# A norm's rows of roots and its sums of squares, moved behind other products on TensorE in a two-block transformer kernel

## The reference

```python
def _rmsnorm(x, gain):
    x32 = x.astype(jnp.float32)
    y = x32 * lax.rsqrt(jnp.mean(x32 * x32, axis=-1, keepdims=True) + NORM_EPS)
    return (y * gain).astype(x.dtype)
...
    for l in range(DEPTH):
        h = h + 0.5 * _swiglu(_rmsnorm(h, ffn1_norm[l]), ffn1_w_gate[l], ffn1_w_up[l], ffn1_w_down[l])
        h = h + _hybrid_mixer(_rmsnorm(h, mix_norm[l]), w_in[l], ...)
        h = h + 0.5 * _swiglu(_rmsnorm(h, ffn2_norm[l]), ffn2_w_gate[l], ffn2_w_up[l], ffn2_w_down[l])
```

## Time and profile before

| | |
|---|---|
| median of three runs | 3609.88 us (3608.93 to 3610.8) |
| the profiled execution, its own time | 3611.69 us |
| its span | 3609.8 us |
| TensorE matmul busy | 3382.9 us, 94% |
| VectorE busy | 1724.0 us, 48% |
| ScalarE busy | 1338.8 us, 37% |
| DMA | 288.05 MB, mean 80 GB/s |
| TensorE's mean granted clock | 0.967 of full speed |

### The profile page before, as it was taken

The page is one execution under the profiler, slowest core; times in us unless marked ns, Lnnn a source line. Parts: engine busy times, 40 slices in busy tenths (PEclk is TensorE's granted clock), DMA queues, the critical chain, the costliest instruction groups (busy, mean ns, idle before and its releaser), DMA issues.

```text
span 3609.8 us, 38935 instructions
## 1 busy us (share of the span) xinstructions
PE 3382.9 (94%) x15366; PEld 2744.1 (76%) x15366; DVE 1724.0 (48%) x2415; ACT 1338.8 (37%) x1897; POOL 30.5 (1%) x62
## 2 busy tenths in 40 slices
PE   8999988799999999998979999988999998999998
PEld 6888765687888888876668788877777776778887
DVE  4443454654443444344465444454445466544433
ACT  4332334343322333233434333344444456433322
POOL 0000000000000000000000000000000000000000
PEclk9999999999999999999989999998999999999999
DMA  4333211112333233322111232321211222233332
GB/s 139 100 91 98 93 59 53 32 45 90 99 93 99 91 98 96 98 83 64 55 31 42 94 99 91 97 76 41 65 47 59 71 90 72 87 102 96 100 92 66
DMA packets 107396, 288.05 MB, mean 80 GB/s; under 512 B 22912, under 2 KB 34176, under 8 KB 107216
## 3 DMA queue, kind: packets, MB, share of 16 engines
q1 hardware_dynamic: 91696, 278.70, 25.0%
q10 hardware_dynamic: 14208, 2.63, 0.4%
q0 software_dynamic: 1312, 4.25, 0.4%
HBM read 282.64 MB, written 2.88 MB: 79 GB/s over the span
## 4 chain that ended last, share of the span: by engine, by line
PE 77%; DVE 11%; ACT 9%; issue 3%; DMA 1%; ACTq 0%; DVEq 0%; SPq 0%
PE ps L722 23%; PE ps L724 22%; PE ps L723 22%; DVE wl L1830 3%; ACT wh L1289 3%; DVE mf L2014 2%; PE ps L731 2%; PE ps L1029 1%; PE ps L1024 1%; PE ps L1185 1%; DVE mf L2024 1%; PE ps L736 1%; PE ps L1167 1%; PE ps L1181 0%; ACT mf L1423 0%
## 5 line engine op out<-in xcount | busy, mean ns | idle before, releaser
L1830 DVE TENSOR_TENSOR wl<-raw,wh 128x1024 fp32r<-128x1024 f32 (+2 forms) x581 | 652.3, 1123 | 1428.1 <-ACT wh L1289 1426.4
L722 PE MATMUL ps<-hnh,wh 128*128 128x512 f32 x2712 | 1095.7, 404 | 35.5 <-DVE mf L2478 10.7
L723 PE MATMUL ps<-hnl,wh 128*128 128x512 f32 x2712 | 1070.6, 395 | 0.0
L724 PE MATMUL ps<-hnh,wl 128*128 128x512 f32 x2712 | 1070.0, 395 | 0.0
L1289 ACT ACTIVATE wh<-raw 128x1024 fp32r<-128x1024 f32 (+2 forms) x581 | 566.9, 976 | 1073.9 <-PE ps L724 1046.0
L722 PEld LDWEIGHTS ps<-hnh,wh 128*128 128x128 f32 x2712 | 520.0, 192 | 167.8 <-issue 25.5
L724 PEld LDWEIGHTS ps<-hnh,wl 128*128 128x128 f32 x2712 | 518.0, 191 | 111.3
L723 PEld LDWEIGHTS ps<-hnl,wh 128*128 128x128 f32 x2712 | 520.0, 192 | 108.3 <-issue 4.0
L722 PE MATMUL ps<-mr,wh 128*128 128x512 f32 x1300 | 514.2, 396 | 24.9 <-DVE h L1956 9.1
L723 PE MATMUL ps<-mr,wh 128*128 128x512 f32 x1300 | 509.3, 392 | 0.0
L724 PE MATMUL ps<-mr,wl 128*128 128x512 f32 x1300 | 509.2, 392 | 0.0
(11 more groups left out here) (324 smaller groups left out, 2558.0 us busy)
## 6 DMA issues: line engine op xcount, KB each, us to landing
raw<-in_w_in SPq DMA_DIRECT2D x140, 512.0 KB, 3.5
raw<-in_ffn_w_gate SPq DMA_DIRECT2D x88, 512.0 KB, 3.5
raw<-in_ffn_w_up SPq DMA_DIRECT2D x88, 512.0 KB, 3.5
raw<-in_ffn_w_down SPq DMA_DIRECT2D x64, 512.0 KB, 3.5
raw<-in_w_ffn_in SPq DMA_DIRECT2D x44, 512.0 KB, 3.5
raw<-in_ffn_w_down SPq DMA_DIRECT2D x32, 384.0 KB, 3.1
raw<-in_w_out SPq DMA_DIRECT2D x32, 256.0 KB, 2.7
raw<-in_w_out_ssm SPq DMA_DIRECT2D x32, 256.0 KB, 2.5
```

The costliest lines, as they stand in the source:

```text
L722: self.e.matmul(out, ah, bh, start=start, stop=False, skip_group_check=shared)
L723: self.e.matmul(out, ah, bl, start=False, stop=False, skip_group_check=shared)
L724: m = self.e.matmul(out, al, bh, start=False, stop=stop, skip_group_check=shared)
L1830: self.e.tensor_tensor(lo[:, 0:n], k.raw[u % NRAW][:, 0:n], hi[:, 0:n].bitcast(F), ALU.subtract).then_inc(k.w_lo, 1)
```

## The change

Only TensorE's stream changes. `rstd` no longer issues the rows; it notes that they are due (`rows_due`), and `product` issues them (`root_rows`) when the next product has done its first two k-tiles, six matmuls. And where the stage's products have fewer than eight k-tiles (`short`), `sums(0)` is issued right ahead of `sums(1)`, behind the next stage's first product. The norm with two roots keeps both as they were.

```diff
@@ product
-        for _ in self.pieces(xs, ready, bank):
+        for n, _ in enumerate(self.pieces(xs, ready, bank)):
             self.beside()
+            if n == 1:
+                self.root_rows()
@@ run_late
-            if i >= 6:
-                self.sums(i - 6)
+            if i == 6 and not self.short:
+                self.sums(0)
             if i == 7:
+                if self.short:
+                    self.sums(0)
+                self.sums(1)
                 if self.r == LAST:
                     self.two_roots()
                 else:
@@ add_h_all
         self.r += 1
+        self.short = len(xs) < 8
@@ rstd of TensorE
-        self.wait_ge(*k.rs_v.at(self.rs_n(), "cols"))
-        self.rows_of(k.ps[B_RSTD], k.rc, k.rs_p.up(self.rs_n(), "rows"))
+        self.rows_due = self.rs_n()
+
+    def root_rows(self):
+
+        k, n = self.k, self.rows_due
+        if n is not None:
+            self.rows_due = None
+            self.wait_ge(*k.rs_v.at(n, "cols"))
+            self.rows_of(k.ps[B_RSTD], k.rc, k.rs_p.up(n, "rows"))
```

More of the change, by code:

```diff
@@ L297, in __init__ @@
         self.gates_done, self.prepared = {}, []
+        self.short, self.rows_due = False, None
         self.qk_took, self.v_took = {}, {}
@@ L397, in h_new @@
         self.late = i
+    def root_rows(self):
+        pass
     def run_late(self):
```

## The result

The changed kernel took 3583.28 us in the median of four runs (3580.01 to 3587.13), the kernel before beside it 3609.4 us; the ratio is 0.9928, with a 95% interval from 0.9911 to 0.9945. The forecast was 3589.2 us and its range began at 3584.0, so the direction was right and the gain, 26.1 us, larger than the 20.6 forecast and 0.7 us outside the range. The interval of the ratio stands for a gain of 20 to 32 us, so it takes in the forecast gain. Over all fourteen runs the median is 3586.1 us, against 3609.7 for 67 runs of before that stood beside these and the other kernels: 23.6 us.

What follows compares the result with a forecast made beforehand. TensorE was taken to bound the kernel, with 77% of the chain that ended last. 2 x 6.48 + 2 x 2.89 + 2 x 0.95 = 20.6 us off 3609.88 gave 3589.2 us; range 3584 to 3598 us.

Steps and rivals of the forecast that it cites:

- The long places: Two FFN stages behind products of twenty-two k-tiles: 2.89 us gain each, 1.48 work put into the pause, 1.41 clock.
- the 1.41 of the clock: Long FFN places: 1.41 us each, the clock staying up as the pause shrinks from 2.21 to 0.86 us.
- The short places: Before each layer's second FFN, behind products of four k-tiles: 6.48 us gain each, 13.0 for the two.
- the first rival: The clock falls all the same, 1.52 us a fall; 11.0 us off the gain, 3600.2 us; chance 0.12.
- The mixers: At two mixers only the earlier copy of the roots counts: 0.95 us each, 1.9 in all; ends 0 and 2.89.
- rival 3: The mixers pass on all of TensorE's gain: 2 x 1.94 us more, 3585.3 us; chance 0.08.
- the sum: Whole kernel: gains at two short stages, two long stages and two mixers add to 20.6 us, giving 3589.2 us.
- 2 us for each unknown term: Allowance round the forecast time, used to set the range from 3584 to 3598 us.
- Rivals 2: Short stages: the next product cannot start at 823.30, for weights or a hidden wait; 7.2 us less, 3596.4 us; chance 0.08.
- 4: Short stages and mixers win nothing, a later wait takes it back; 5.8 us left, 3604.1 us; chance 0.05.
- 5: At six places the clock stays at 1.2 GHz for the whole second product; 12 us slower, 3622 us; chance 0.03.
- theory A: Follow-up expectation: the extra gain comes from stretches the change doesn't touch, by the clock, up to 5 us either way.

Runs made afterwards that it cites:

- the filler: Kernel before, nothing moved, sixteen passes of unused matmuls in the pause between sums and rows at all six places: 3600.61 us against 3609.27, ratio 0.9976.
- the rows at the long places: Kernel before with the rows of roots moved at the two long FFN places only: 3601.44 us, ratio 0.9980.
- the sums only: Changed kernel with all rows right behind the second sums again, so only the short stages' first sums are moved: 3603.7 us against 3610.7, ratio 0.9981.
- before begun later: Kernel before with 1.6 us of unused matmuls added at its start: 3609.76 us against 3609.27, ratio 1.0000.

## Why the prediction was right or wrong

**The long places: right.** 2.89 us forecast, 2.78 and 2.99 measured, the same within 0.02 us in three executions. The split held too: the filler kept the clock up and gave 1.43 and 1.61 us for the 1.41 of the clock. The pause left before the rows was 0.70 us instead of 0.86.

**The short places: mechanism right, with the first rival in half of the cases.** 6.48 us forecast, 6.3 measured where the clock stays up, 4.7 where it falls behind the two sums. Of six short places in three profiled executions three were of each kind (364.72, 364.51 and 364.49 us against 366.30, 366.10 and 366.23). The forecast had the fall as a rival that strikes everywhere or nowhere (3600 us); it strikes at single places, for 1.6 us each, and it begins behind the sums, after up to three matmuls, and takes in the rows that follow. Its evidence against that rival, 1.00 between 820 and 825 us, was read where no sums stand.

**The mixers: mechanism right, size too small.** The copy of the roots starts 4.35 us behind the second sums instead of 5.26: 0.91 us for the 0.95 forecast, and TensorE's wait for VectorE grew as said. Moving the rows there alone gave 1.7 us for the 1.9 forecast. In the traces of the changed kernel, however, the mixers are 2.4 to 2.7 and 3.5 to 5.8 us shorter. In the second one a pause of 4.07 us was followed by the low clock (a matmul of 0.80 us at 1592.37), and it lasted for all twelve matmuls up to a small one (L736) on which VectorE waits:

```profile
1597.23 0.63 PE L724 MATMUL ps<-hnh,wl 128*128 128x512 f32 x1
1597.79 0.41 PE L736 MATMUL ps<-cst,mf 4*128 4x4 f32 x4
```

Now two shorter pauses stand there, and the matmul behind the second has 0.50. The first execution:

```profile
1568.42 0.50 PE L732 MATMUL ps<-hnh,wh 128*128 128x512 f32 x1 [3.13 <-DVE mf L2008]
...
1578.22 0.50 PE L732 MATMUL ps<-hnh,wh 128*128 128x512 f32 x1 [2.46 <-DVE mf L2008]
...
1582.63 0.50 PE L746 MATMUL ps<-cst,mf 4*128 4x4 f32 x4
```

And the second:

```profile
1581.51 0.50 PE L732 MATMUL ps<-hnh,wh 128*128 128x512 f32 x1 [1.33 <-DVE mf L2008]
...
1584.45 0.41 PE L746 MATMUL ps<-cst,mf 4*128 4x4 f32 x4
```

From the end of the pause to the small matmul it is 5.42 us in before, 4.41 in the first execution, with seven slow matmuls, and 2.94 in the second and third, with none. With the 0.91 us of the copy that makes 1.9 and 3.4 us, and the last eviction by L1991 of before comes just so much earlier: 68.1 us behind the second sums in before, 66.3 and 64.7 in the changed kernel. So this part of the extra is the clock behind the second pause, which the forecast priced at nothing. It goes with an earlier copy of the roots: that eviction comes at 66.8 us at the latest in every kernel in which the clock was up at that mixer's rows, and the copy so 0.5 to 0.9 us earlier (with moved rows, with the filler, and in the rows at the long places, where nothing was moved there), and at 68.2 and 68.3 in the two others in which it fell. Why the earlier copy is followed by fewer slow matmuls is not shown. It is rival 3 in a small way. In the first mixer the last of these evictions comes 0.9 us earlier (60.4 for 61.3), just as forecast. In the first execution that lead has shrunk to 0.3 us at 297 us behind the second sums, and it grows to 2.7 over the last 110 us, far from what was moved.

**The step that failed** is the sum, 2 x 6.48 + 2 x 2.89 + 2 x 0.95, which puts all that stands between and behind the places at nothing, and the range's "2 us for each unknown term", which gives it no room either. The mixers' term, 0.95 us each, is the one that came out too small in the traces (2.4 to 2.7 and 3.5 to 5.8 us); the parts in which nothing was moved gave 5.6 us more in the first execution and about 0 and 2.5 in the others. Mixers with the code of before took 425.3 to 431.4 us (second) and 425.5 to 428.8 (first), and the second block, whose code is the same in all kernels, 848.8 to 853.2. In before's own profile the second mixer had the longest length seen. Against such a profile the kernels with its code won 5.0 us there in the sums only, 4.6 in before begun later, and 6.1 in the rows at the long places. Their whole times do not show it: beside their own places (6.4, 0 and 5.8 us) the medians leave 0.7, nothing and 1.6 us, so other parts and other runs take it back. Over fourteen runs the changed kernel is 23.6 us faster, 3.0 more than forecast; the other 2.5 us of the first median are scatter between groups of four or five runs, whose medians were 3583.3, 3588.7 and 3586.4. The second and third of them lie inside the range. That the first lay 0.7 us outside it is thus partly the luck of four runs, on top of an extra that the forecast did not have.

**Rivals 2, 4 and 5** did not happen: the product started 0.74 us behind its bank, the saved time stayed, and no changed place showed more than eight slow matmuls. In the FFN stages no product waited for its bank behind the rows. The root starts 1.30 us behind the start of the table load in the changed kernel too, had 1.29. The Trainium skill, page "ScalarE: Activation LUTs", section "What ACT_TABLE_LOAD costs", adds a drain of about 1380 ns to the load at every switch of the set. This trace does not show it: at the long place the load starts 0.01 us behind the work before it and the root 0.02 us behind the load's end.

**What stays open** is what sets whether a pause is followed by the low clock and for how long. The runs show the same pause with three different lengths behind it. The kernel before repeats its parts within 0.1 us in two executions, all but the start; the changed kernel does not (its second mixer took 425.99, 425.60 and 427.87 us). So neither the program nor chance alone has been shown to decide. No run varied the moment alone in small steps, which would settle it. Open too is the second block: it took 849.04 and 851.91 us in two executions of the changed kernel at the same mean granted clock, 0.96, so theory A's "by the clock" is not shown for it.

## What to carry to other kernels

Where one small operation waits for a chain over two other engines, put it behind as much of the next product as covers the chain. At the long places half of the win was the work that fills the pause, the other half the clock that no longer falls. Price the places that you change from rows, but give the whole time a margin for the untouched parts too: here the two mixers and the second block differed by 3.3, 6.1 and 4.5 us between kernels that have the same code there, which is more than the uncertainty of the change's own places. A gain of a few us in such a kernel needs the trace cut into parts, since runs of one program differ by 10 us, while in the changed kernel the long places repeat within 0.02 and the short ones take one of two lengths. It needs more than one trace of each kernel as well: a single one may be of its fastest or slowest run.

## What the runs showed of the hardware that was not expected

- The same 3.02 us pause at the end of the second mixer was followed by 5.7 us, 3.4 us or none at a granted 1.2 GHz, in kernels that differ only ahead of it.
- A pause of 3.13 us was followed by a matmul at 2.4 GHz (0.50 us) in one execution of the changed kernel and by one at 1.2 GHz (0.80 us) in another, while one of 2.21 us behind the sums was followed by the low clock at all four places of before, in both of its profiled executions; in two other kernels one such place each stayed up.
- Two sums of one-column matmuls, 1.7 us, with short pauses ahead, let the clock fall at half of the six places that the changed kernel's traces show, and then behind the first or third matmul of the next product. The Trainium skill, page "TensorE: Matmul & The Clock Gate", section "A second HAM failure mode: psum-queue depth-cycling", tells of a clock that swings where small idle times stand between groups of matmuls; here a fall and rise of that kind costs 1.6 us a place.
- After a wait of 3.3 to 3.5 us for the first sums at a short place, the unchanged product behind them had seven matmuls at 1.2 GHz in before, and up to thirteen in other kernels with the same code there.
- Sixteen passes of unused matmuls in a pause brought 1.4 to 1.6 us per long place: keeping TensorE busy with nothing was worth as much as six matmuls of real work moved there.
